# Handover from the up weights to the down weights of a PEER layer: four edits to the order of work

## What is computed

```python
def chunk(args):
    hc, ec, gc = args
    u = peer_u[ec]
    a = jax.nn.gelu(jnp.einsum("ckd,cd->ck", u, hc).astype(jnp.float32)) * gc
    vv = peer_v[ec]
    return jnp.einsum("ck,ckd->cd", a.astype(vv.dtype), vv)
```

## Time and profile before

| | |
|---|---|
| median of 3 runs | 3043.14 us |
| the runs | 3035.45, 3043.56, 3043.14 us |
| span of the profiled execution | 3035.8 us |
| own time of the profiled execution | not given apart from its span |
| up stage ends, down stage starts on PE | 2471.4 us, 2484.8 us of the span |

### The profile page before, as it was taken

The page is one execution under the profiler, slowest core; times in us unless marked ns, Lnnn a source line. Parts: engine busy times, 40 slices in busy tenths (PEclk is TensorE's granted clock), DMA queues, the critical chain, the costliest instruction groups (busy, mean ns, idle before and its releaser), DMA issues.

```text
span 3035.8 us, 37322 instructions
## 1 busy us (share of the span) xinstructions
PE 2851.3 (94%) x13639; PEld 2375.3 (78%) x13639; DVE 2261.9 (75%) x3023; ACT 1483.0 (49%) x1990; POOL 600.4 (20%) x480
## 2 busy tenths in 40 slices
PE   5989987999999999999999989999999989999998
PEld 3657756888888768776777779899999978888887
DVE  6465547888888852887854339999998768888886
ACT  3443236788887743544542433463656633333332
POOL 0200111111111000000000000033234434444442
PEclk7999998999999999999999999999999999999999
DMA  7544636999999833332333334487778999999995
GB/s 299 169 157 160 207 117 238 368 370 367 360 358 353 299 104 120 108 115 81 101 128 139 123 124 162 165 307 282 257 281 320 359 376 351 364 365 367 359 368 185
DMA packets 203628, 746.30 MB, mean 246 GB/s; under 512 B 24752, under 2 KB 78128, under 8 KB 146352
## 3 DMA queue, kind: packets, MB, share of 16 engines
q1 hardware_dynamic: 124656, 497.12, 45.5%
q0 software_dynamic: 56912, 179.26, 16.9%
q10 hardware_dynamic: 21872, 67.48, 5.8%
HBM read 670.80 MB, written 98.11 MB: 253 GB/s over the span
## 4 chain that ended last, share of the span: by engine, by line
PE 52%; DVE 17%; issue 7%; DMA 5%; ACT 3%; ACTq 0%; DVEq 0%; POOL 0%; SPq 0%; POOLq 0%
PE PS L549 45%; DVE wlo L1896 3%; DMA gbuf<-in_peer_u_dram,IDX 3%; DVE hf L2665 2%; DVE oh L2651 2%; ACT whi L1226 1%; DVE hf L2677 1%; PE PS L1016 1%; PE PS L1028 1%; PE PS L855 1%; ACT HH L1866 1%; DMA ht<-in_peer_u_dram,IDX 1%; PE PS L1150 1%; DVE cand L2619 1%; DVE cand L2616 1%
## 5 line engine op out<-in xcount | busy, mean ns | idle before, releaser
L1896 DVE TENSOR_TENSOR wlo<-raw,whi 128x2048 fp32r<-128x2048 f32 x392 | 894.6, 2289 | 340.0 <-ACT whi L1226 302.0
L1226 ACT ACTIVATE whi<-raw 128x2048 fp32r<-128x2048 f32 x392 | 751.2, 1917 | 360.2 <-PE PS L549 305.0
L549 PE MATMUL PS<-HH,whi 128*128 128x512 f32 (+1 forms) x2056 | 792.4, 385 | 38.8 <-DVE wlo L1896 18.9
L549 PE MATMUL PS<-HH,wlo 128*128 128x512 f32 (+1 forms) x2056 | 755.5, 367 | 0.0
L549 PE MATMUL PS<-HL,whi 128*128 128x512 f32 (+1 forms) x2056 | 754.5, 367 | 0.0
L549 PEld LDWEIGHTS PS<-HH,whi 128*128 128x128 f32 x2056 | 393.7, 191 | 100.5 <-DVE wlo L1896 22.0
L549 PEld LDWEIGHTS PS<-HL,whi 128*128 128x128 f32 x2056 | 393.7, 192 | 46.4 <-issue 7.7
L549 PEld LDWEIGHTS PS<-HH,wlo 128*128 128x128 f32 x2056 | 392.6, 191 | 43.4
L549 PE MATMUL PS<-whi,HH 128*128 128x512 f32 (+1 forms) x896 | 352.6, 393 | 22.4 <-DVE HL L2707 17.0
L549 PE MATMUL PS<-wlo,HH 128*128 128x512 f32 (+1 forms) x896 | 347.8, 388 | 0.0
L549 PE MATMUL PS<-whi,HL 128*128 128x512 f32 (+1 forms) x896 | 347.8, 388 | 0.0
(11 more groups left out here) (429 smaller groups left out, 3942.3 us busy)
## 6 DMA issues: line engine op xcount, KB each, us to landing
raw<-in_moe_dram SPq DMA_DIRECT2D x192, 1024.0 KB, 7.4
raw<-in_u_units_dram SPq DMA_DIRECT2D x64, 1024.0 KB
raw<-in_v_units_dram SPq DMA_DIRECT2D x64, 1024.0 KB
raw<-in_w_in_dram SPq DMA_DIRECT2D x44, 1024.0 KB
raw<-in_w_ada_dram SPq DMA_DIRECT2D x24, 1024.0 KB, 20.1
acts_dram<-sS ACTq DMA_DIRECT2D x64, 384.0 KB
gates_dram<-XT ACTq DMA_DIRECT2D x24, 1024.0 KB
sS<-acts_dram SPq DMA_DIRECT2D x42, 384.0 KB
```

The costliest lines, as they stand in the source:

```text
L549: ins = t.matmul(dst, a, b, start=(first and n == 0), stop=(last and n == 2))
L1226: a.inc(a.e.activation(m.whi[p % HRING][:, :, :], m.raw[RAW_SLOT[load_of(p)]][:, :, :], ACT.Copy), "hi", p)
L1896: v.inc(v.e.tensor_tensor(m.wlo[h][:, :, :], m.raw[RAW_SLOT[load_of(p)]][:, :, :], m.whi[h][:, :, :].bitcast(F32), ALU.subtract), "lo_v", p)
```

## The change

1. `LAST_GATE` goes from 121 to 118 and `LAST_ROW` from 126 to 124; the planner places the last gate step at n = 118 instead of 120 and row 115 at n = 124 instead of 126, and `OPEN` becomes 59 instead of 60.
2. DVE multiplies the first activations (`gate_acts(0)`) at the start of its list for n = 127, ahead of the split of v1, with the waits for `open` and the gates' writes ahead of that. ACT's high half of them moves ahead of the gelu of n = 127. SP issues `acts(0)` ahead of its wait for the last writes of the gates and of `gates(0)`.
3. The halves of the first unit go to columns 0 to 127 of chunks 0 to 5 of `HH` and `HL`, which the up stage does not read, and ACT no longer waits for the end of step 127 on PE for them.
4. PE's first pass of the down stage takes token tiles 3, 1, 2 and waits for each of banks 0 to 3 by itself (gelu of 124 to 127), and for banks 4 and 5 for the gate steps.

```diff
-LAST_GATE, LAST_ROW, UP_ROWS = 121, 126, 116
+LAST_GATE, LAST_ROW, UP_ROWS = 118, 124, 116

+FIRST_TILES = (3, 1, 2)
+
+def first_slot(ci, i):
+
+    return (NT - TD // 128) * ci + i - TD // 128
+
+def gated_halves(m, u):
+
+    if u == 0:
+        return [x[:, 0:2 * NT - 2 * (TD // 128), 0:TD] for x in (m.HH, m.HL)], m.sA[0][:, :, :].rearrange(
+            "p c (i t) -> p (c i) t", t=TD)
+    k = u % 4
+    return [x[:, 2 * k:2 * k + 2, TD:] for x in (m.HH, m.HL)], m.sA[u % 3][:, :, :]

 def pe_peer(pe, m):
...
-            for i in range(TD // 128, NT):
+            for i in (FIRST_TILES if u == 0 and ci == 0 else range(TD // 128, NT)):
...
                     if u == 0 and ci == 0:
-                        pe.wait_ge("act", 127)
-                        pe.wait_ge("gput", N_GATE - 1)
+                        if bank < 4:
+                            pe.wait_ge("act", 124 + bank)
+                        else:
+                            pe.wait_ge("gput", N_GATE - 1)
                     o = 1024 * ci + 512 * half
-                    s = slice(128 * i, 128 * i + 128)
-                    ins = mm3(t, m.PS[:, bank, :], m.HH[:, 2 * k + ci, s], m.HL[:, 2 * k + ci, s], wh[:, o:o + 512],
+                    if u == 0:
+                        kc, s = first_slot(ci, i), slice(0, TD)
+                    else:
+                        kc, s = 2 * k + ci, slice(128 * i, 128 * i + 128)
+                    ins = mm3(t, m.PS[:, bank, :], m.HH[:, kc, s], m.HL[:, kc, s], wh[:, o:o + 512],

 act_peer
+    def prepare(u):
+        (high, _), src = gated_halves(m, u)
+        a.wait_ge("gated", u)
+        if u:
+            a.wait_ge(*(("down", u - 4) if u >= 4 else ("up", 127)))
+        a.inc(s.activation(high, src, ACT.Copy), "ahi", u)
+
     for n in range(128):
         u, ci = divmod(n, 2)
         if ci == 0:
             act_high(a, m, FIRST["u_units"] + u + HRING - 1)
+        if n == 127:
+            prepare(0)
...
-    def prepare(u):
-        k = u % 4
-        a.wait_ge("gated", u)
-        a.wait_ge(*(("down", u - 4) if u >= 4 else ("up", 127)))
-        a.inc(s.activation(m.HH[:, 2 * k:2 * k + 2, TD:], m.sA[u % 3][:, :, :], ACT.Copy), "ahi", u)
-
-    prepare(0)

 dve_peer
+    def gate_acts(u):
...
+    def low_acts(u):
+        (high, low), src = gated_halves(m, u)
+        v.wait_ge("ahi", u)
+        v.inc(e.tensor_tensor(low, src, high.bitcast(F32), ALU.subtract), "alo", u)
+
     for n in range(128):
+        if n == 127:
+            v.wait_all("open")
+            v.wait_ge(f"gate5_out{(N_GATE // 4 - 1) % 2}", N_GATE // 4 - 1)
+            v.wait_ge(f"gate5_out{N_GATE // 4 % 2}", N_GATE // 4 - 2)
+            gate_acts(0)
         if n % 2:
             dve_low(v, m, FIRST["u_units"] + n // 2 + HRING - 1)
...
-    v.wait_all("open")
-    v.wait_ge(f"gate5_out{(N_GATE // 4 - 1) % 2}", N_GATE // 4 - 1)
-    v.wait_ge(f"gate5_out{N_GATE // 4 % 2}", N_GATE // 4 - 2)
...
-    prepare(0)
+    low_acts(0)
     for u in range(64):
         dve_low(v, m, FIRST["v_units"] + u + HRING - 1)
         if u + 1 < 64:
-            prepare(u + 1)
+            gate_acts(u + 1)
+            low_acts(u + 1)

 sync_program
     y.wait_all("open")
+    acts(0)
     y.wait_ge(f"gate5_out{(N_GATE // 4 - 1) % 2}", N_GATE // 4 - 1)
     y.wait_ge(f"gate5_out{N_GATE // 4 % 2}", N_GATE // 4 - 2)
     gates(0)
-    acts(0)
```

More of the change, by code:

```diff
@@ L2683, in dve_peer @@
     e = v.e
-    for n in range(128):
+    def gate_acts(u):
+        i, g, k = u % 3, u // 4, u % 4
+        v.wait_ge(f"acts_in{i}", u)
+        v.wait_ge(f"gates_in{g % 2}", g)
+        sa = bass.AP(m.sA[i], 0, [[2 * TDN, 128], [TDN, 2], [16, NG], [1, 16]])
+        v.inc(e.tensor_tensor(sa, sa, bass.AP(m.Gin[g % 2], 32 * k, [[m.GSTR[g % 2], 128], [16, 2], [128, NG], [1, 16]]),
+                              ALU.mult), "gated", u)
+    def low_acts(u):
+        (high, low), src = gated_halves(m, u)
+        v.wait_ge("ahi", u)
+        v.inc(e.tensor_tensor(low, src, high.bitcast(F32), ALU.subtract), "alo", u)
+    for n in range(128):
+        if n == 127:
[3 more added lines that the diff above has]
+            gate_acts(0)
         if n % 2:
```

## The result

The changed kernel takes 3043.38 us (median of 20 runs, 3040.95 to 3049.81) beside 3040.31 for the kernel before (20 runs, 3035.45 to 3045.45): a ratio of 1.0014, 95% interval 1.0008 to 1.0020. It is slower by 0.1 to 0.2%, inside the 0.3% named in the prediction, and on the other side of the forecast. The profiled execution took 3042.38 us, its span is 3040.6.

A forecast was written before the change was run, and what follows sets the result against it. The up stage's end on DVE was taken to be set by DMA bytes for rows. v1's first matmul at 2492.5 instead of 2495.5 took 3.0 us off the 3043.1 median, giving 3040, range 3029 to 3047.

The forecast's parts named there:

- What bounds the kernel: Up stage's end: DVE late behind rows waiting for DMA bytes; PE's handover gap 13.4 plus slow clock 2.5, 15.9 us in all.
- Gates sooner: SP's gates(0) before the handover: its mark stays at row 107, so the earlier gate steps gain nothing.
- unused columns: First unit's halves on ACT: the wait removed had long been met; worth nothing, 0.5 us at most.
- single banks: PE's first down pass waiting bank by bank: worth nothing, 0.5 us at most if rows come early.
- Rows sooner: DVE's rows before the handover: row 115 read out at 2476.7 instead of 2479.7, 3.0 us sooner, bounds 0 and 9.
- The stall in the up stage: PE before step 126: u63's split, now behind row 112, makes PE stand still 6.4 us; the stall moves.
- The gap before v0: Handover: row 115, two splits, gating and low half in series give first down matmul at 2483.1, gap of 5.3 us.
- The next wait: Before v1: its activations, acts(1), gated 7.27 us behind v1's split as before, at 2489.4; v1's matmul at 2492.5.
- The clock: PE around the handover: gaps of 6.4 and 5.3 may or may not lower it; slow start puts v0's end at 2493.8, not 2491.3.
- the second rival: Handover: row 115 stays at 2479.7, v1 at 2495.5, nothing gained, 3043, or 1.2 us more; chance 0.15.
- the third: Down stage: late splits bunch loads on SP's queue, acts(1) lands 12 us behind the split, 9 us slower, 3052; chance 0.08.

The follow-up runs named there:

- rows108_before: The kernel before with UP_ROWS 108 instead of 116, so eight rows move to the down stage: a gain of 0.26%.
- early_rows108_oldcols: Changed kernel with UP_ROWS 108 and acts(1) ahead of v4's load, but parts 3, 4 and ACT's share of part 2 undone: 3032.47 us.
- rest_only: The changed kernel with the old LAST_GATE 121 and LAST_ROW 126, parts 2 to 4 kept: 0.9984 to 1.0001 of the kernel before.
- acts1_early: The changed kernel with SP issuing acts(1) ahead of v4's load: 0.15% or 4.6 us under the changed kernel by the ratios.
- planner_only: The kernel before with LAST_GATE 118 and LAST_ROW 124 alone: 0.9998 to 1.0018 of the kernel before.
- acts1_early_before: The kernel before with acts(1) issued ahead of v4's load: no change of time, A to v1 6 us shorter in a single profile.

## Why the prediction was wrong

**What bounds the kernel** was right: DVE stood behind rows, the rows behind DMA bytes. rows108_before shows it: take 4.2 MB away ahead of the handover and the gap goes.

**Gates sooner, unused columns, single banks: nothing.** Right for this kernel. gates(0) left behind row 107 at 2456.17; and the columns and banks show only in early_rows108_oldcols, with the rows out of the way.

**Rows sooner.** Forecast: row 115 read out at 2476.7, 3.0 us sooner. The profile had 2475.7, the second about 2482.0. Counted from A the two are 6.3 us sooner and not at all (297.4 and 303.7, against 303.7 and 303.2). Their mean fits the 3.0, by luck: rest_only, without the planner's numbers, has 300.9 as well, so no run shows that a deferred load brought the rows forward. Row 105, behind which u61's split had gone, even came later: its dot is 269.8 us behind A before, 272.5 and 272.9 in the changed kernel.

**The stall in the up stage.** Right that it moves there, wrong in place and size: before step 122, 4.3 us, not before 126, 6.4. I priced only the split of u63 and never checked that of u61, which had gone behind row 105.

**The gap before v0.** The series came out: 2482.05 from row 115's 2475.7, 6.35 us where the sum had 6.42. The gap itself was 2.1 and 8.0 us where the sum had 5.3, since it depends on when row 115 comes.

**The next wait.** This is the step that failed: "DVE gated them at 2489.23 after waiting for the DMA, 7.27 us behind that split's end ... Now ... gating is at 2489.4". I carried the 7.27 us over. It had v5's load right ahead of acts(1) (2481.98 and 2482.42), but v4's 11.4 us earlier (2471.03). In the changed kernel v4's load goes out at 2478.04, v5's at 2481.11 and acts(1) at 2481.54, all within 3.5 us, and the gating came 13.5 us behind that split's end at 2481.08, at 2494.55; in the second profile 9.8 us. With the planner's numbers alone it was 9.8 and 10.3; with the old ones 7.3, 7.4 and, in rest_only, 8.2; with v5's load moved behind acts(1), 7.1. The same deferred megabyte had been counted as room for the rows and was not charged where it went.

What that did to v1, counted from A: in the first profile its split ended 3.4 us sooner than forecast and its activations were 6.2 us late, in the second the split ended 2.9 us later and the activations were 2.6 us late. So v1 began 2.8 and 5.5 us behind the forecast, and the 3.0 us of gain became 0.2 of gain and 2.4 of loss. The price of acts(1) is not the whole cause: where it was taken away (acts1_early), v1 came no sooner, 320.5, because rows and loads were late instead. The sum of PE's gaps was 13.6 and 14.2, where the forecast had 6.4 + 5.3 + 1 = 12.7.

**The clock.** Left open at 0 to 2.5 us and taken as no more than before. Both profiles of the changed kernel have two falls of it around these gaps for one. In the first they cost 3.6 us, in the second 3.3 (1.7 on step 122, and 1.6 on v0, whose first 8 matmuls took 3.42 us), the one large gap 2.5.

The outcome is the second rival, "the stall only moves", which had 0.15; the starved activations of the third were there too, at a lower price than its 9 us. The range, 3029 to 3047, took the time in, but the way was wrong, and that it lies in the range says nothing for the mechanism. The difference of 3.1 us between the medians is not fully found in the profiles: from A to the last down matmul the changed kernel needs 845.6 and 845.9 us, the kernel before 843.2 and 845.1, so 1.6 us more in the mean of two. Up to A both kernels have the same lists, and A lies anywhere from 2173.5 to 2181.7 in the span, 7.9 us apart in the two profiles of planner_only, so single profiles can't show where the rest is. It stays open.

## What to carry to other kernels

In a stretch that was full on DMA, the edits that moved waits and issues about shortened it by 3 us at most and usually not at all, except in the one profile of acts1_early_before; moving bytes out shortened it by 13. So count the bytes that have to pass ahead of the point in question, and move bytes to a place that has room. A transfer that an edit defers has to be charged again where it lands, to whatever is issued behind it on its queue. Look for the gain in the sum of the engine's gaps from a fixed point before to a fixed point behind, not in the gap that was aimed at.

## What the runs showed that I had not expected

A gap of 2.10 us before v0 left TensorE's clock up; those of 4.34, 7.16 and 13.38 came with a fall to its lower level. Splitting one idle time in two cost clock. But the length of the last gap does not decide it alone. In the same execution a gap of 2.11 us, with only the 8 small matmuls of a gate step (1.05 us) in front of it, was followed by a fall, and so was the gap of 2.3 us at A in every profile but rest_only's, where the same gap (2.27) between the same matmuls was followed by none. What decides it stays open. PE, then two stretches of it, changed kernel:

```profile
2221.46 1.05 PE L1150 MATMUL PS<-oh 128*128 128x128 f32 x8
2224.62 1.55 PE L1150 MATMUL PS<-oh 128*128 128x128 f32 x8 [2.11 <-ACT XT L1824]
```

```profile
2224.60:2225.15 0.55, 0.53 (x5) 0.55 (x6) 0.55 (x1) 0.55 (x3) 0.00 (x0) 1.00 0.86 335
2225.20:2228.55 3.35, 3.35 (x14) 3.35 (x14) 3.35 (x3) 1.51 (x5) 2.28 (x1) 0.50 0.43 89
```

The price of a row is not the same on both sides. Ahead of the handover 8 rows fewer gave 12.9 us in the kernel before, 1.6 us a row. In the down stage the first 6 to 8 cost 1 to 5 us in all, the next 4 cost 9 (527.4 to 536.3, one profile). The DMA share did not tell the two cases apart: in the stretch above it was 1.04 with 108 rows, where PE hardly waited, and 1.02 with 104.
